# Attention of an encoder block: the value products of two query chunks in one run every second step

## What is computed

```python
def attend(qb):                    # qb: one chunk of 128 queries
    s = jnp.einsum('bqhd,bkhd->bhqk', qb, k, preferred_element_type=jnp.float32) * scale
    p = jax.nn.softmax(s, axis=-1).astype(v.dtype)
    return jnp.einsum('bhqk,bkhd->bqhd', p, v)
o = lax.map(attend, q_blocks)      # 8 chunks of the prompt, 2 of the sample, for each head
...
return o @ w_b_out
```

## Time and profile before

| | |
|---|---|
| median of three runs | 2090.97 us (2090.43 to 2091.37) |
| profiled execution, time on the device | 2090.73 us |
| its span from first to last instruction | 2089.0 us |
| PE busy | 2039.4 us, 98% of the span |
| DVE busy | 1353.8 us, 65% |
| ACT busy | 950.4 us, 45% |
| POOL busy | 904.5 us, 43% |
| attention, steps 0 to 83 | from about 713 to 1073 us |

### The profile page before, as it was taken

The page is one execution under the profiler, slowest core; times in us unless marked ns, Lnnn a source line. Parts: engine busy times, 40 slices in busy tenths (PEclk is TensorE's granted clock), DMA queues, the critical chain, the costliest instruction groups (busy, mean ns, idle before and its releaser), DMA issues.

```text
span 2089.0 us, 33205 instructions
## 1 busy us (share of the span) xinstructions
PE 2039.4 (98%) x13240; PEld 1680.9 (80%) x13240; DVE 1353.8 (65%) x1629; ACT 950.4 (45%) x1188; POOL 904.5 (43%) x640
## 2 busy tenths in 40 slices
PE   8999999999999999999999999799999999999997
PEld 7888888888788788888888887677777777777775
DVE  7864455456777477777754358876676667766774
ACT  7112211113555366666631033455556555555563
POOL 0975555566655376666642601412222222222221
PEclk9999999999999999999999999899999999999999
DMA  4223544334677522222134432688887778888873
GB/s 151 104 104 132 164 165 147 114 89 132 234 255 242 204 64 87 87 96 66 56 110 156 158 141 82 237 352 313 314 298 287 277 284 313 312 312 312 299 284 106
DMA packets 168937, 398.98 MB, mean 191 GB/s; under 512 B 16512, under 2 KB 88192, under 8 KB 168832
## 3 DMA queue, kind: packets, MB, share of 16 engines
q1 hardware_dynamic: 154096, 344.43, 45.0%
q0 software_dynamic: 7680, 20.98, 4.5%
q10 hardware_dynamic: 7056, 32.12, 4.3%
HBM read 318.19 MB, written 79.30 MB: 190 GB/s over the span
## 4 chain that ended last, share of the span: by engine, by line
PE 84%; DVE 9%; ACT 3%; POOL 2%; issue 1%; DMA 0%; ACTq 0%; DVEq 0%; SPq 0%; POOLq 0%
PE PS L1619 25%; PE PS L419 13%; PE PS L420 13%; PE PS L421 13%; PE PS L1650 8%; PE PS L1402 3%; DVE topi L2651 1%; PE PS L1389 1%; PE PS L1393 1%; PE PS L1390 1%; PE PS L1391 1%; PE PS L1392 1%; PE PS L1332 1%; DVE topv L2649 1%; DVE work L2653 1%
## 5 line engine op out<-in xcount | busy, mean ns | idle before, releaser
L419 PE MATMUL PS<-act_hi,w_hi 128*128 128x256 f32 (+1 forms) x800 | 274.9, 344 | 7.5 <-DVE act_lo L2226 3.2
L420 PE MATMUL PS<-act_lo,w_hi 128*128 128x256 f32 (+1 forms) x800 | 269.7, 337 | 0.0
L421 PE MATMUL PS<-act_hi,w_lo 128*128 128x256 f32 (+1 forms) x800 | 269.2, 336 | 0.0
L981 POOL TENSOR_SCALAR prob<-prob,small 128x1024 f32<-128x1024 f32 (+1 forms) x80 | 200.5, 2506 | 123.3 <-DVE small L2539 123.3
L1051 POOL DMA_INDIRECT y_s<-ob_s,ixs_s x16 | 43.8, 2738 | 353.6 <-DVE ob_s L2810 353.6
L419 PEld LDWEIGHTS PS<-act_hi,w_hi 128*128 128x128 f32 x800 | 151.5, 189 | 25.0 <-DVE act_lo L2226 3.6
L1619 PE MATMUL PS<-ehi,xT_hi 128*128 128x512 f32 x520 | 165.5, 399 | 0.8 <-DVE xT_lo L2724 0.6
L421 PEld LDWEIGHTS PS<-act_hi,w_lo 128*128 128x128 f32 x800 | 151.2, 189 | 16.4
L420 PEld LDWEIGHTS PS<-act_lo,w_hi 128*128 128x128 f32 x800 | 151.6, 190 | 14.7 <-issue 0.7
L1619 PE MATMUL PS<-elo,xT_hi 128*128 128x512 f32 x520 | 160.6, 390 | 0.0
L1619 PE MATMUL PS<-ehi,xT_lo 128*128 128x512 f32 x520 | 160.4, 390 | 0.0
(11 more groups left out here) (375 smaller groups left out, 5466.9 us busy)
## 6 DMA issues: line engine op xcount, KB each, us to landing
raw<-in_w_gate SPq DMA_DIRECT2D x64, 1024.0 KB, 8.5
raw_more<-in_w_up SPq DMA_DIRECT2D x32, 1024.0 KB, 12.0
raw_w<-in_w_up SPq DMA_DIRECT2D x32, 1024.0 KB, 16.7
w_raw<-in_w_in SPq DMA_DIRECT2D x16, 1024.0 KB, 7.0
w_raw<-in_w_down SPq DMA_DIRECT2D x15, 1024.0 KB
stg<-in_w_down SPq DMA_DIRECT2D x15, 1024.0 KB, 7.7
gt<-in_w_down SPq DMA_DIRECT2D x15, 1024.0 KB, 12.9
raw_end<-in_w_down SPq DMA_DIRECT2D x15, 1024.0 KB, 14.6
```

The source lines that it names most:

```text
L419: pe.matmul(out, lh, rh, start=first, stop=False)
L420: pe.matmul(out, lh, rl, start=False, stop=False)
L421: return pe.matmul(out, ll, rh, start=False, stop=last)
L981: pool.tensor_scalar(prob[:, n % 3, 0:kn], prob[:, n % 3, 0:kn], prec[:, s:s + 1], None, ALU.mult).then_inc(S["norm_pool"], 1)
```

## The change

In the even steps PE no longer issues any value products. In the odd steps it issues both halves of the pair, one behind the other, at the place where only the second half stood. The number and kind of the instructions are the same, and so is the order on ACT, DVE, POOL and SP.

```diff
                 if 2 <= n < STEPS + 2:
                     turn_prob(n - 2)
-                if n >= 4:
-                    values((n - 4) // 2, n % 2)
+                if n >= 5 and n % 2:
+                    for half in range(2):
+                        values((n - 5) // 2, half)
                 if 4 <= n and h < H - 1 and s < PIECES:
                     turn_head(PIECES * (h + 1) + s)
```

## The result

The changed kernel takes 2103.09 us (median of 6 runs, 2101.58 to 2104.03) against 2090.93 us of the kernel before in the same comparison (6 runs, 2089.32 to 2091.59). The ratio is 1.0058, with a 95% interval from 1.0048 to 1.0068: slower by 12.2 us; the forecast was 2103.5.

What follows compares the result with a forecast made beforehand. PE was taken to bound the attention, with bank 4's reading as a fixed latency. Terms 8.5 + 1.4 + 2.7 = +12.6 us gave a span of 2101.6 and a median of 2103.5, range 2098.5 to 2108.

Steps and rivals of the forecast that it cites:

- The floor of 3.53 us: On PE, a chunk's transpositions cannot follow a prompt chunk's sooner than 3.53 us, until ACT and DVE have read bank 4.
- The pieces of PE's own work: PE's costs: eight transpositions 0.87 us, four 0.44, two 0.22; half run of value products 1.44; scores 2.30, sample's 0.60.
- T(8) to T(9): Interval from the transpositions of the chunk at place 8 to those at place 9: 5.08 us before, 3.61 forecast.
- The wait inside the interval: Between transpositions at places 2 and 3: about 1.6 us idle PE, before the next head's transpositions or before place 3's.
- T(2) to T(3): Interval between transpositions at places 2 and 3, with the sample's short scores: stays 3.53 us; PE's work there only 1.91.
- The loop at places 6 to 9: DVE and ACT nearly their own loop: transpositions at places 4 to 7 keep 12.69 us, 7 to 8 keep 4.00.
- Six heads, first head, last head: Added attention time: +8.5 us for six heads at +1.42 each, +1.4 first head, +2.7 last head and drain.
- Behind the attention: After the attention: the shift is carried to the end; the clock at 1300 to 1350 us plays 2 us either way.
- The short steps: Rival, steps without value products: they cost nothing, about -4 us, 2087; chance 2%, with other ways to gain 3%.
- The loop did not loosen: Rival at places 6 to 9: PE reaches 12.19 and 3.89 us, -4 us, 2099; chance 10% alone.
- No normalization was late at T(9): Rival: POOL's normalization delays place 9's transpositions in each head, +6 us, 2110, chance 6%; last head alone +2, 2105.5.
- The clock did not fall: Rival at place 4: PE at 1.2 GHz for the 24 products, 2.88 us more a head, +23, 2126; chance 3%.

Runs made afterwards that it cites:

- e6: Changed kernel with both halves of a pair's value products in the even step, none in the odd steps: 2111.48 us, ratio 1.0101.
- e3: Changed kernel with PS banks 4 and 5 signalled and read in two halves by ACT and DVE: 2091.56 us, ratio 1.0003.
- e7: Changed kernel without ACT's high copy and DVE's low part of the rotary queries for heads 2 to 7: 2099.38 us, ratio 1.0048.
- e5: Changed kernel without DVE's low part of the rotary queries for heads 2 to 7, ACT's copy kept: 2103.43 us, ratio 1.0061.
- e4: Kernel before the change with PS banks 4 and 5 signalled and read in two halves: 2084.09 us against 2091.18, ratio 0.9967.

## Why the prediction was right

**The floor of 3.53 us.** Right, and it is the cause. The interval is 3.50 to 3.53 with value products in it, without them, one step earlier (e6), and in the drain; reading the bank in halves moves it to 2.40, and to 2.11 where DVE is free (e3).

**The pieces of PE's own work.** Right within 0.01 us an interval on the head shown: 3.62, 6.50, 4.80 and 6.32 measured for 3.61, 6.49, 4.79 and 6.32. In the other heads T(8) to T(9) is up to 3.66. That merging saves nothing at the turn from transpositions to products came out too: PE's busy time in the attention moved by 0.2 us in 364.

**The wait inside the interval.** T(2) to T(3) was forecast with an idle time of about 1.6 us "before H or before T". By the starts it is 3.50 less 1.91, so 1.59; the rows show 1.24 of it as idle, 0.19 before H and 1.05 before T(3). H now follows T(2) at once and meets the low part of the next head's keys, which DVE has ready 1.08 us after the start of T(2). It comes that way because the copy of the pair on ACT waits 0.60 us for the end of the run of 24, and the high part of the keys stands behind it:

```profile
955.79 0.38 ACT L2049 ACTIVATE ostg<-PS 128x256 f32<-128x256 f32 x1 [0.60 <-PE PS L421]
956.23 0.69 ACT L1998 ACTIVATE k_hi<-PS,small 128x512 fp32r<-128x512 f32 x1
...
956.95 0.75 DVE L2483 SCALAR_TENSOR_TENSOR k_lo<-PS,small,k_hi 128x512 fp32r<-128x512 f32 x1 [1.56 <-ACT k_hi L1998]
```

The prediction looked at this chain at place 7 and said that nothing is late. Behind T(2) it is late: H starts 1.23 us after T(2), where 0.87 would do. That costs nothing, since the floor holds there either way. All of PE's waits for these low parts are 16.5 us, where 15 to 20 had been forecast.

**The loop at places 6 to 9.** The forecast kept 12.69 and 4.00 against 12.19 and 3.89 of PE's work, and 12.70 and 3.99 were measured. The prediction called it a loop of DVE and ACT that holds the rotary parts; e7 shows it. It did not say through which branch it runs: two of them end together, and the first experiment on it took one away and left the other (e5).

**Six heads, first head, last head.** 1.39 a head measured on the one shown, between 1.38 and 1.43 in all six, 8.5 together, as forecast; 1.5 in the first head for 1.4; 2.7 in the last head and the drain for 2.7. T(2) and T(3) of the first head are 3.53 apart in both kernels. The whole attention is 12.6 us longer, by the sum 12.6. The span moved by 11.8 only, because the attention of this profiled execution began 0.8 us earlier than that of the kernel before (712.67, 713.47); between all the traces this start lies from 711.4 to 714.4 us, with nothing changed ahead of it. The median moved by 12.2, and the 0.4 between it and the sum is less than the spread of the runs.

**Behind the attention.** The shift is carried to the end in full: 1016.1 us in both kernels.

**The rivals.** The short steps did cost: 12 us. The loop did not loosen by itself. No normalization was late at T(9): it ended at 941.39, 0.43 before T(9) at 941.82, the margin forecast as 0.4 (0.34 to 0.47 in the other heads, and 1.4 in the last).

```profile
938.54 2.85 POOL L981 TENSOR_SCALAR prob<-prob,small 128x1024 f32<-128x1024 f32 x1 [1.14 <-DVE small L2540]
```

In the last head one was late already in the kernel before, which the prediction did not see: there POOL's 4.01 us end just before T(3), and T(2) to T(3) is 4.13 us.

```profile
1036.26 1.06 PE L1402 MATMUL PS<-ident,prob 128*128 128x128 f32 x8 [0.44 <-DVE pt_lo L2533]
...
1040.39 1.09 PE L1402 MATMUL PS<-ident,prob 128*128 128x128 f32 x8 [1.03 <-POOL prob L981]
```

The forecast put the bare floor of 3.53 there without asking for POOL. It came out (3.49), with the normalization ending 0.27 us before T(3), less than the 0.4 that the prediction called its smallest margin. That part was luck.

The clock did not fall: it is granted in full over the attention, and also over the ten us around place 4 that hold T(2), the waits and the run of 24:

```profile
955.00:965.00 10.00, 8.75 (x71) 8.24 (x70) 5.55 (x13) 5.74 (x13) 7.62 (x4) 1.00 0.05 16
```

The Trainium skill (TensorE: Matmul & The Clock Gate, "Part 4: PE-mode transpose") says that transpositions do not count as busy PE in the same way as products. That gave no loss here, where 20 transpositions, five short products and 1.2 us of idle time stand together. Whether a longer stretch of them would let the clock fall is open; no run had one.

**More gain than three waits in e4.** The gain of 6.8 us is more than the three waits a head that its expectation named. The traces of the two kernels give it by parts: the six heads are 4.5 us shorter together, the first head is 1.4 shorter (T(1) to T(2) 2.11 us in place of 3.51), the last head 0.4 and the last interval of the drain 0.5.

**What stays open.** With the bank read in halves, merging costs 8.1 us of attention (360.7 against 352.6): 5.6 in the six heads, 1.4 in the first head, 1.1 in the last head and the drain. Of the 5.6, 2.9 are T(2) to T(3) above PE's own work and 0.65 is the one wait for a load; the rest was not taken apart by a run.

## What to carry to other kernels

Count, behind each fill of a single-buffered accumulator bank, what its readers need until it is free, and lay PE's other work so that every interval between two fills holds at least that much; a sum over two steps says nothing, since what one interval has too much does not help the next. An interval with little work of its own (here the sample's short scores) is the one that must keep its filling. Where the filling doesn't suffice, let the readers hand the bank back in parts: signalling by PS bank took the floor from 3.50 to between 2.11 and 2.40 us for 0.05 to 0.06 us more on each reader, and made the kernel before 0.33% faster.

## What had not been expected of the hardware

Two reads of 512 columns cost hardly more than one of 1024: 1.09 against 1.03 us on ACT and 1.28 against 1.23 on DVE, where 0.1 us for each half had been allowed. And wherever PE waited for "low", the gap between its end and PE's next start was 0.14 to 0.15 us in the seven traces without halves, whatever stood between, so in this kernel the floor could be read to 0.03 us from one place and used in all heads.
